# Attention of a two-layer trunk, scheduled by heads instead of pairs of heads, with the softmax scale applied after the value product

## The reference, cut to what matters

```python
q = (rms_norm(c_q, g_q) @ w_uq).reshape(B, S, MLA_HEADS, MLA_QK_DIM)      # 16 heads, 64 + 32 wide
kv = (rms_norm(c_kv, g_kv) @ w_ukv).reshape(B, S, MLA_HEADS, MLA_NOPE_DIM + MLA_V_DIM)
for blk in range(S // ATTN_BLOCK):                                         # 4 blocks of 128 queries
    s = (einsum(q_n, k_n[:, :k_end]) + einsum(q_r, k_r[:, :k_end])) * scale
    s = jnp.where(k_idx[None, :] <= q_idx[:, None], s, -jnp.inf)
    p = jax.nn.softmax(s, axis=-1)
    outs.append(jnp.einsum('bhqk,bkhd->bqhd', p, v[:, :k_end]))
return concatenate(outs) @ w_o
```

## Time and profile before

| what | value |
|---|---|
| median of 3 executions | 1282.24 us (1276.78 to 1285.5) |
| the profiled execution | 1280.36 us |
| its span, first to last instruction | 1278.6 us |
| TensorE busy | 1220.6 us, 95% of the span |
| VectorE busy | 665.7 us, 52% |
| ScalarE busy | 456.3 us, 36% |
| GpSimd busy | 268.5 us, 21% |
| TensorE's granted clock, mean | 0.985 |

### The profile page before, as it was taken

The page is one execution under the profiler, slowest core; times in us unless marked ns, Lnnn a source line. Parts: engine busy times, 40 slices in busy tenths (PEclk is TensorE's granted clock), DMA queues, the critical chain, the costliest instruction groups (busy, mean ns, idle before and its releaser), DMA issues.

```text
span 1278.6 us, 15796 instructions
## 1 busy us (share of the span) xinstructions
PE 1220.6 (95%) x5822; PEld 1009.0 (79%) x5822; DVE 665.7 (52%) x957; ACT 456.3 (36%) x727; POOL 268.5 (21%) x245
## 2 busy tenths in 40 slices
PE   7989999899999999999999998889999999999996
PEld 6767777778888888888888986667888888888885
DVE  6778888544434334344467544985453443443432
ACT  5346666433212212123342235653231221221242
POOL 2312232232102102012201134552120120110221
PEclk9989999899999999999999998989999999999998
DMA  5210101133233232322224221012323223232211
GB/s 183 46 27 23 27 23 49 66 99 99 99 99 99 99 98 98 99 87 89 91 67 132 91 91 50 25 42 66 99 99 99 91 90 112 72 108 92 94 67 66
DMA packets 113887, 104.00 MB, mean 81 GB/s; under 512 B 20934, under 2 KB 112164, under 8 KB 113836
## 3 DMA queue, kind: packets, MB, share of 16 engines
q1 hardware_dynamic: 113804, 103.29, 25.4%
q10 hardware_dynamic: 32, 0.01, 0.0%
HBM read 101.17 MB, written 2.11 MB: 81 GB/s over the span
## 4 chain that ended last, share of the span: by engine, by line
PE 79%; DVE 8%; issue 6%; ACT 3%; POOL 2%; DMA 1%; DVEq 0%; ACTq 0%; POOLq 0%; SPq 0%
PE ps L1479 24%; PE ps L1481 24%; PE ps L1480 24%; DVE nmax L1122 2%; POOL xl L583 1%; DVE xl L981 1%; DVE qtmp L1114 1%; ACT prob L725 1%; ACT uh L739 1%; DVE rinv L1127 1%; ACT whi L640 1%; DMA x_tok<-in_x 1%; DVE diag L1395 1%; ACT xh L711 1%; PE ps L1534 0%
## 5 line engine op out<-in xcount | busy, mean ns | idle before, releaser
L976 DVE TENSOR_TENSOR wlo<-raw,whi 128x2048 fp32r<-128x2048 f32 (+3 forms) x89 | 194.5, 2189 | 157.8 <-ACT whi L640 157.8
L1479 PE MATMUL ps<-xl,whi 128*128 128x512 f32 (+1 forms) x688 | 270.1, 393 | 0.2 <-issue 0.2
L640 ACT CAST whi<-raw 128x2048 fp32r<-128x2048 f32 (+4 forms) x150 | 184.8, 1260 | 239.3 <-PE ps L1481 234.8
L1480 PE MATMUL ps<-xh,whi 128*128 128x512 f32 (+1 forms) x688 | 267.8, 389 | 0.0
L1481 PE MATMUL ps<-xh,wlo 128*128 128x512 f32 (+1 forms) x688 | 267.8, 389 | 0.0
L1479 PE MATMUL ps<-ul,whi 128*128 128x512 f32 x608 | 237.2, 390 | 1.2 <-POOL wlo L531 1.2
L1481 PE MATMUL ps<-uh,wlo 128*128 128x512 f32 x608 | 236.6, 389 | 0.0
L1480 PE MATMUL ps<-uh,whi 128*128 128x512 f32 x608 | 236.5, 389 | 0.0
L561 POOL TENSOR_TENSOR ul<-sq,uh 128x512 fp32r<-128x512 f32 x64 | 83.6, 1307 | 521.3 <-ACT uh L828 521.3
L1204 DVE TENSOR_TENSOR h<-ps,h 128x512 f32<-128x512 f32 x80 | 55.0, 690 | 197.1 <-PE ps L1481 192.5
L1479 PEld LDWEIGHTS ps<-xl,whi 128*128 128x128 f32 (+1 forms) x688 | 128.6, 187 | 28.9 <-issue 2.1
(11 more groups left out here) (242 smaller groups left out, 1628.5 us busy)
## 6 DMA issues: line engine op xcount, KB each, us to landing
raw<-in_mlp_w SPq DMA_DIRECT2D x64, 1024.0 KB, 5.1
raw<-in_mlstm_w_in SPq DMA_DIRECT2D x12, 1024.0 KB, 5.2
raw<-in_mla_w_o SPq DMA_DIRECT2D x4, 1024.0 KB, 4.7
raw<-in_mlstm_w_o SPq DMA_DIRECT2D x4, 1024.0 KB, 4.9
raw<-in_mla_w_in SPq DMA_DIRECT2D x3, 1024.0 KB, 5.7
raw<-in_mla_w_uq SPq DMA_DIRECT2D x16, 192.0 KB, 2.4
x_tok<-in_x SPq DMA_DIRECT2D x4, 512.0 KB, 8.1
mb<-m_rows SPq DMA_DIRECT2D x8, 256.0 KB, 3.2
```

The lines of the kernel that those rows point to most:

```text
L640: last = sc.copy(hi, src)
L976: last = v.tensor_tensor(lo, src, hi.bitcast(F32), ALU.subtract)
L1479: mm(o, ah, bl, start=first, stop=False)
L1480: mm(o, ah, bh, start=False, stop=False)
```

## The change

The step is now a head. The loops of PE, ACT, DVE and POOL over pairs are written out for all 16 heads (SP's loop stays). A third PSUM bank is given to the scores, and `prob` keeps all four blocks of a head. The probabilities are no longer scaled: the transposes take them right after `exp`. `vh` and `vl` get 64 columns of zeros between the two heads' values, so that a head's product has its values in its own 64 rows and zeros in the other's, and both heads add up in one bank. The reciprocals of a pair's row sums are made once in a pair (`row_scales`, DVE), turned (`turn_scales`, PE; `rows_turned`, ACT), spread over the rows by four matmuls with a constant `pick` (`spread_scales`, PE; `rows_spread`, ACT), and DVE multiplies the pair's value product by them (`o_scaled`). Its split is now ACT's `o_high` and POOL's `o_low`. The value product of a head runs in the next head's step, ahead of that step's second half of `q_half` and its third turn. `vh` of a pair is cast by ACT at the end of the pair's even step.

```diff
-B_Q, B_KV, B_S, B_PT, B_PV = 0, 1, 2, 4, 6
+B_Q, B_KV, B_S, B_PT, B_PV = 0, 1, 2, 5, 7
+S_RING = 3
...
-        return q_mm, n - N_PAIR + 1
+        head = n - N_PAIR
+        return (q_mm, head + 1) if head % 2 or head == 0 else (k_mm, head // 2 + 1)
...
+            for head in range(3):
+                strip_low(N_PAIR + head, "q" if head % 2 else "kq")
+            for head in range(HEADS):
+                if head == 0:
+                    v_low(0)
+                if head % 2 and head > 1:
+                    o_low(head // 2 - 1)
+                if head + 3 < HEADS:
+                    strip_low(N_PAIR + head + 3, "kq" if head % 2 else "q")
+                elif head + 3 < HEADS + 2:
+                    strip_low(N_WO + head + 3 - HEADS, "full")
+                if head and head % 2 == 0:
+                    v_low(head // 2)
...
+            def exp(head, b):
+                z = 4 * head + b
+                act.wait_ge(s_max, z + 1)
+                if head:
+                    act.wait_ge(t_mm, z - 3)
+                sc.activation(prob_of(b), ps[:, B_S + z % S_RING, 0:P * (b + 1)], ACT.Exp,
+                              bias=nmax[:, b:b + 1],
+                              accum_out=rsum[:, 4 * (head % 2) + b:4 * (head % 2) + b + 1]).then_inc(s_exp, 1)
...
+            def attention(head):
+                i, second = head // 2, head % 2
+                nxt = head + 1 < HEADS
+                if second:
+                    if nxt:
+                        for e in range(2):
+                            k_high(e, i + 1)
+                    if i:
+                        o_high(i - 1)
+                elif i == 0:
+                    v_high(0)
+                pt_high(head, 0)
+                pt_high(head, 1)
+                if head + 3 < HEADS:
+                    split(N_PAIR + head + 3, "q" if not second else "kq")
+                elif head + 3 == HEADS:
+                    split(N_WO)
+                if second:
+                    rows_turned(i)
+                pt_high(head, 2)
+                if nxt:
+                    exp(head + 1, 0)
+                pt_high(head, 3)
+                if nxt:
+                    exp(head + 1, 1)
+                if head + 2 < HEADS:
+                    q_high(head + 2)
+                if nxt:
+                    exp(head + 1, 2)
+                    exp(head + 1, 3)
+                if second:
+                    rows_spread(i)
+                elif i:
+                    v_high(i)
+                if head + 2 == HEADS:
+                    split(N_WO + 1)
...
+            def row_scales(i):
+                dve.wait_ge(s_exp, 8 * i + 8)
+                if i:
+                    dve.wait_ge(rt_mm, i)
+                own.link(v.reciprocal(rinv[:], rsum[:]))
+                own.link(v.tensor_copy(rinv2[:, 0:8], rinv[:]))
+                low(rinv2[:, 8:16], rinv[:], rinv2[:, 0:8]).then_inc(r_inv, 1)
...
+            def o_scaled(i):
+                dve.wait_ge(w_mm, 2 * i + 2)
+                dve.wait_ge(r_ready, i + 1)
+                if i >= 2:
+                    dve.wait_ge(o_lo, i - 1)
+                v.tensor_tensor(o_norm(i), bank(B_PV), r_b[:], ALU.mult).then_inc(o_new, 1)
...
+            def attention(head):
+                nxt = head + 1 < HEADS
+                i, second = head // 2, head % 2
+                if second:
+                    if i:
+                        o_scaled(i - 1)
+                    row_scales(i)
+                if second and nxt:
+                    for e in range(2):
+                        k_low(e, i + 1)
+                pt_low(head, 0)
+                pt_low(head, 1)
+                if head + 2 < HEADS:
+                    q_table(head + 2)
+                if nxt:
+                    row_max(head + 1, 0)
+                pt_low(head, 2)
+                if nxt:
+                    row_max(head + 1, 1)
+                    row_max(head + 1, 2)
+                pt_low(head, 3)
+                if nxt:
+                    row_max(head + 1, 3)
+                if head + 2 < HEADS:
+                    q_low(head + 2)
...
+            def weigh(head):
+                e = head % 2
+                cols = slice(VD * e, VD * e + P)
+                pe.wait_ge(t_hi, 4 * head + 4)
+                pe.wait_ge(v_hi, head // 2 + 1)
+                if e == 0 and head:
+                    pe.wait_ge(o_new, head // 2)
+                for j in range(TT):
+                    mm(ps[:, B_PV, P * j:S], vh[:, j, cols], pth[e][:, j, P * j:S], start=(e + j == 0), stop=False)
+                pe.wait_ge(v_lo, head // 2 + 1)
+                for j in range(TT):
+                    mm(ps[:, B_PV, P * j:S], vl[:, j, cols], pth[e][:, j, P * j:S], start=False, stop=False)
+                pe.wait_ge(t_lo, 4 * head + 4)
+                for j in range(TT):
+                    last = mm(ps[:, B_PV, P * j:S], vh[:, j, cols], ptl[e][:, j, P * j:S], start=False,
+                              stop=(e == 1 and j == TT - 1))
+                last.then_inc(w_mm, 1)
+            def turn_scales(i):
+                pe.wait_ge(r_inv, i + 1)
+                if i < PAIRS - 1:
+                    pe.wait_ge(k_lo, 2 * i + 4)
+                tr(ps[0:16, b_row(i), 0:P], rinv2[:].bitcast(F32), ident[:]).then_inc(rt_mm, 1)
+            def spread_scales(i):
+                pe.wait_ge(rt_ready, i + 1)
+                if i == 0:
+                    pe.wait_ge(pick_ready, 1)
+                for b in range(TT):
+                    last = mm(ps[:, b_row(i), P * b:P * b + P], pick[:, b, :], rt[:], start=True, stop=True)
+                last.then_inc(r_mm, 1)
...
+            def attention(head):
+                ahead = head + 2 < HEADS
+                if ahead:
+                    q_half(head + 2, 0)
+                turn_p(head, 0)
+                turn_p(head, 1)
+                if head:
+                    weigh(head - 1)
+                if ahead:
+                    q_half(head + 2, 1)
+                if head % 2:
+                    turn_scales(head // 2)
+                turn_p(head, 2)
+                scores(head + 1, 0)
+                scores(head + 1, 1)
+                turn_p(head, 3)
+                scores(head + 1, 2)
+                scores(head + 1, 3)
+                if head % 2:
+                    spread_scales(head // 2)
+                elif ahead:
+                    k_product(head // 2 + 1)
+            def attention_end():
+                head = HEADS - 2
+                turn_p(head, 0)
+                turn_p(head, 1)
+                weigh(head - 1)
+                scores(head + 1, 0)
+                scores(head + 1, 1)
+                turn_p(head, 2)
+                out_products(range(0, 1))
+                turn_p(head, 3)
+                scores(head + 1, 2)
+                scores(head + 1, 3)
+                out_products(range(1, 2))
+                head = HEADS - 1
+                turn_p(head, 0)
+                turn_p(head, 1)
+                weigh(head - 1)
+                turn_scales(head // 2)
+                out_products(range(2, 3))
+                turn_p(head, 2)
+                out_products(range(3, 4))
+                turn_p(head, 3)
+                out_products(range(4, 5))
+                spread_scales(head // 2)
+                weigh(head)
+                out_products(range(5, KD))
```

More of the change, by code:

```diff
@@ L718, in exp @@
[L718 to L732, removed]
@@ L742, in _ @@
             c_high(2, cq, cqh, G_Q, 4)
             for e in range(2):
-                k_high(e, 0, 0)
+                k_high(e, 0)
             split(N_PAIR + 1, "q")
[L746 to L794, removed]
+            q_high(0)
+            q_high(1)
+            split(N_PAIR + 2, "kq")
+            for b in range(TT):
+                exp(0, b)
+            def attention(head):
[5 more added lines that the diff above has]
+                            k_high(e, i + 1)
+                    if i:
+                        o_high(i - 1)
[26 more added lines that the diff above has]
+                    split(N_WO + 1)
@@ L796, in residual_stage @@
+            for head in range(HEADS):
+                attention(head)
+            o_high(PAIRS - 1)
             def residual_stage(n0, t0, norm, gain):
@@ L1193, in _, with q_low, row_max @@
-            attention(0, first=True)
-            with dve.Fori(1, PAIRS - 1) as i:
-                own.enter(i, 1, 8)
-                attention(i)
-                own.leave(1, PAIRS - 1)
-            attention(PAIRS - 1, last=True)
-            o_low(PAIRS, -1)
+            def q_low(head):
+                dve.wait_ge(q_hi, head + 1)
+                low(ql[head % 2], qtmp[:], qh[head % 2]).then_inc(q_lo, 1)
+            def row_max(head, b):
+                z = 4 * head + b
+                dve.wait_ge(s_mm, z + 1)
+                v.tensor_reduce(nmax[:, b:b + 1], ps[:, B_S + z % S_RING, 0:P * (b + 1)], op=ALU.max, axis=AX.X,
```

(25 more changed lines are left out.)

325 lines of the change are left out of this document (118 added, 207 removed).

## The result

| | before | after |
|---|---|---|
| median | 1282.3 us (1276.78 to 1285.5, 6 runs) | 1269.2 us (1267.67 to 1272.24, 6 runs) |
| ratio | 1 | 0.9902, 95% interval 0.9876 to 0.9927 |
| span of the profiled execution | 1278.6 us | 1265.9 us |
| DVE busy | 665.7 us | 631.5 us |
| TensorE busy | 1220.6 us | 1218.8 us |

The change takes about 1% off, 13.1 us of the median. Of the 12.7 us of the span, 10.95 lie ahead of the point that the prediction compared.

A forecast was written before the change was run, and what follows sets the result against it. PE was taken as bound by 2.9 us of waits a pair for full, in-order DVE, plus tail stops. Start to 94.5, steps 1 to 13 119.2, tail to 245.7: 13.6 us off, 1268 us, range 1258 to 1281.

The forecast's parts named there:

- the point that the prediction compared: Start of the tiles of strip `N_WO + 1`, at 259.27 us before; all after it was taken as untouched.
- The sum: Start, steps and tail together: tiles at 245.7 instead of 259.27 us, 13.6 us off, a median of 1268.
- the tiles: Tiles of strip `N_WO + 1`, after the attention's tail; their start was forecast at 245.7 us.
- The pair: Two heads' steps: even step 9.63 us, odd step 8.77, a pair 18.4 against 20.7.
- The late `vl`: Odd step: `weigh` waits 0.2 us for `vl`, which comes after the last `exp`, `v_high` and `v_low`.
- The last rival: Odd steps: `vl` later than forecast, gain gone from 1.9 us a pair over forecast, 1291 to 1308 us; chance 0.12.
- The cover: Even step: `exp` of block 0 over at 6.8 us, scores 3 start at 7.3, 0.5 us to spare.
- The start: From `q_half` of head 0, ending at 74.8, through step 0, with half clock, to 94.5 us.
- The tail: From step 14: `vl` at 231.0, PE stopped 7.5 us in head 14's product, 1.9 for half clock, end at 245.7.
- Smaller waits: Rival for the pairs: half of the 2.9 us of waits stays, 1.3 us a pair, time 1277 us; chance 0.26.
- The tail was not cheaper: Rival for start and tail: no half clock at the start (2.5), half the tail's wait hidden (3.7), about 1262; chance 0.10.
- the line of 1%: Smallest change a measurement of this kernel can tell from none, 12.8 us; the forecast was said to lie on it.

The follow-up runs named there:

- e4: The kernel before without `normalise`: reciprocals, probability products and the softmax division left out, transposes wait for `exp`, order by pairs kept; 1269.89 us, ratio 0.9899.
- e3: The kernel after with VectorE again doing a one-column reciprocal and a product (by one) over each block of probabilities, transposes waiting for it; 1288.14 us, ratio 1.0045.
- e5: The kernel after with two PSUM banks for the scores instead of three; 1283.55 us, ratio 0.9997.
- e6: The kernel after with `v_low(7)` ahead of the large strip's low part on GpSimd, `pick` built later, `v_high` in the middle of the even step; 1258.37 us, ratio 0.9804.
- e9: e3 with `o_scaled` of a pair moved ahead of the last two products over the probabilities in VectorE's queue; 1292.63 us, ratio 1.0088.
- e7: e6 with one more instruction, an Exp of one column on ACT ahead of the first `q_high`; 1257.17 us, ratio 0.9795.
- e1: The kernel after with GpSimd taking `v_low(7)` ahead of the low part of the large strip `N_WO + 1`; 1261.59 us, ratio 0.9840.
- e8: The kernel before with its attention loops on PE, ACT, DVE and POOL written out, nothing else changed; 1280.65 us, ratio 0.9977.
- e2: The kernel after with GpSimd building the constant `pick` after the low part of strip `N_PAIR` instead of before; 1271.08 us, ratio 0.9910.

## Why the prediction was right, point by point

**The sum.** 13.6 us were forecast up to the tiles, 10.95 measured. Of the 2.6 us between them 0.1 lie ahead of step 1 (which began at 94.62, forecast 94.5), 1.5 in steps 1 to 13 and 1.0 in the tail (step 14 began at 215.35, forecast 213.7). The time came out within 1.2 us of the 1268, partly by luck: the rest of the program was 1.7 us shorter in the profiled execution, and in the eleven kernels it lies anywhere from 1017.6 to 1023.1.

**What bounds it.** That PE waits for an in-order DVE in each pair was right: e4 takes DVE's work out and 2.0 us of the period go, e3 puts it back and they return. The prediction had not asked how much of the gain the order by heads brings, and no run shows it by itself. An estimate: by the prediction's count PE has 17.75 us of work in a pair of e4, and in the kernel after 0.10 for the scales' transpose and 0.59 for the four matmuls more, 18.44. That leaves 1.0 us of waits in e4 and 0.2 in the kernel after. So the order by heads, with the third bank (e5), would hide some 0.8 us a pair more, about what the new work on PE costs.

One reading was wrong. The prediction has DVE at `normalise`, `row_max` and `pt_low` while PE stands for `q_low` up to 107.74. All through that stop, which begins at 106.89, DVE was in `q_low` itself, which POOL's strip held:

```profile
106.45 1.23 DVE L981 TENSOR_TENSOR xl<-qtmp,xh 128x512 fp32r<-128x512 f32 x1
```

```profile
105.43 2.71 POOL L531 TENSOR_TENSOR wlo<-raw,whi 128x256 fp32r<-128x256 f32 x4 [5.84 <-ACT whi L640]
```

Once in each pair it took 1.23 us and once 0.68. In the kernel after no `q_low` of the pairs stands beside a strip:

```profile
L1040 DVE TENSOR_TENSOR xl<-qtmp,xh 128x512 fp32r<-128x512 f32 x12 | 8.3, 690 | 0.0
```

In e4 it still does (1.29 us at 105.27). So the order by heads changed what runs beside `q_low` too, which the prediction did not price.

**The pair.** 18.4 forecast, 18.65 measured, and one term of the period makes up the difference: PE's added work. The four matmuls with `pick` were put at 0.35 us, nearer the upper bound; from the end of the scores to the next `q_half` they take 0.59:

```profile
121.53 0.66 PE L1719 MATMUL ps<-rt,pick 16*128 16x128 f32 x4
122.12 0.51 PE L1654 MATMUL ps<-cql,whi 128*128 128x512 f32 x1
```

So they take 0.15 us each, above my upper bound of 0.11. The late `vl` in the odd step was forecast at 0.2 us. The first low product follows the first high one by 0.80 us there (114.74 to 115.54) and by 0.67 in the even step (123.87 to 124.54): 0.13, and e6, which moves `v_high`, has a period 0.17 shorter.

DVE was forecast at 11.7 us of a pair and had 12.91. 1.0 us of that is the scales' low part of 8 columns, put at 0.16 us: `v_low` holds it to 1.16. The last rival had named this, as costing nothing until 1.3 us is used up, and PE does not wait for it. In e6, where `v_low` comes earlier, DVE has 11.92.

**The cover.** 0.5 us of slack at scores 3 was right: in the kernel after `exp` of block 0 is over at 120.12 and scores 3 begin at 120.64. With one bank less the wait came at the size that e5 expected, 1.4 us a pair.

**The start.** Step 1 began 0.1 us from the forecast, but by errors that cancel. `q_half` of head 1 began at 77.29, forecast 75.8, mostly because `pick` was not priced at all. It stands on POOL beside DVE's `diag`, on the path to the first keys, and cost 1.0 us. Against it, this `q_half` ran wholly at full clock (2.88 us), where 0.8 had been added for half clock, and step 0 took 8.8 us where 7.7 and 1.7 were forecast. The chain from `q_table` of head 1 to step 0 was forecast at 5.5 us from the end of its `q_half` and took 5.6 (80.17 to 85.81). The half clock came a little later than assumed, at 84.9 for 3.4 us.

**The tail.** `vl` was forecast for 231.0 with a wait of 7.5 us, and came at 232.23. From the last high product's work to the low one PE stood for 6.9 us, and 0.65 for `vh` just before. Here the half clock was mis-sized: 1.9 us taken from the 4 us of the earlier trace rows; it lasted from 228.3 to 238.5, 6.3 us of it with PE at work, which costs 3.1.

**The rivals.** The late `vl` did not reach 1.9 us in a pair. Smaller waits did not stay: some 0.2 us a pair are left in all, where that rival had 1.3 more. The tail was not cheaper. The Trainium skill's 215.7 ns for 512 columns, "TensorE: Matmul & The Clock Gate", section "Wait - 56ns, not 53.3ns?", would have put the time at 1258; the period is that of 234 ns, and the row was the better guide.

**The chances.** Of the ratio's interval, 0.9876 to 0.9927, a little less than half lies below 0.99. That the forecast lay on the line of 1% was right.

## What to carry to other kernels

When an in-order engine releases another, ask of each of its operations what stands ahead of it at the moment of need, and what another engine runs beside it. Taking small operations out of DVE's queue won 2 us a pair here with the old order, and the new order hung on one more bank. Price every new instruction, also a constant built once, by what runs beside it on the engine that shares its port. At the end of a pipeline, lay out each queue by hand: the large item of the next stage slips easily ahead of the last small one of this stage.

## What the runs showed of the hardware that I had not expected

An operation of DVE that works in SBUF alone can be held until POOL's instruction beside it ends, however small DVE's own is: the scales' low part, 128x8, has 1.02 us in the mean of seven in the kernel after, and 0.17 us in e3, where POOL is idle beside it.

```profile
L1040 DVE TENSOR_TENSOR rinv<-rinv 128x8 fp32r<-128x8 f32 x7 | 7.1, 1020 | 0.2
```

The Trainium skill, "SBUF - State Buffer", section "SBUF: two separate sides", has this as an exclusive lock of the shared port, for operations of VectorE in a mode with two ports or with two inputs in SBUF; the traces agree, in `diag`, in e3 and in e9. Not every operation on SBUF is held: the reciprocal of one column took 0.16 us at 135.28 in e3, in the middle of `v_low` (135.17 to 136.48), and the product behind it was held.

The granted clock of the mLSTM stage changed by 0.06 between profiled executions of kernels that are the same there. Half clock lay on 17.1 us of that stretch in the four kernels before, after, e6 and e7, whose rest is 1017.6 to 1019.3; on 20.5 in e1, e3, e4 and e8 with 1020.1 to 1021.8; on 30.7 in e2 and e5 with 1023.0 and 1023.1. e9 does not fit the row, with 27.3 and 1020.8. Nor is it a mark of the kernel alone: of 17 executions of the kernel before, one took 1276.95 us at a mean granted clock of 0.989 and another 1285.78 at 0.981, though where in the program these two differ no trace shows. So differences of up to 5 us between profiled executions can come from a stage that no edit touched, and the start of a late stage is the better measure of an edit ahead of it.
